# A hybrid encoder step: ten of eleven down steps of the FFN by seven block products instead of eight

## What is computed

```
h = rmsnorm(x)                              # norm2_g
a = h @ w_up                                # 1024 -> 2 * 2816
a = causal_depthwise_conv(a, width 3)       # prompt and each sample by itself
gate, up = split(a)
x = x + (silu(gate) * up) @ w_down          # 2816 -> 1024
```

## Time and profile before

| | us |
|---|---|
| three runs | 3447.86, 3453.91 (median), 3458.95 |
| profiled execution | 3453.28 |
| its span | 3451.5 |
| mean granted clock of PE | 0.965 |

### The profile page before, as it was taken

The page is one execution under the profiler, slowest core; times in us unless marked ns, Lnnn a source line. Parts: engine busy times, 40 slices in busy tenths (PEclk is TensorE's granted clock), DMA queues, the critical chain, the costliest instruction groups (busy, mean ns, idle before and its releaser), DMA issues. The chain is left out here.

```text
span 3451.5 us, 56818 instructions
## 1 busy us (share of the span) xinstructions
PE 3243.1 (94%) x23942; PEld 3039.6 (88%) x23942; DVE 2001.9 (58%) x3541; ACT 902.0 (26%) x1655; POOL 887.2 (26%) x782
## 2 busy tenths in 40 slices
PE   7999997889999999999988999979899999999997
PEld 5988975779999999999988898648799999999996
DVE  6396564562655565555666855546537655555556
ACT  3244244243211111111233431532332111111112
POOL 3221110223322222222342212011243222222223
PEclk9999998799999999999999999979999999999998
DMA  5633231101111111111164322320011111111111
GB/s 189 193 95 109 85 111 59 67 18 43 42 40 41 43 43 37 44 43 43 36 185 145 100 77 87 112 102 9 29 42 43 43 37 44 43 43 43 37 43 66
DMA packets 123430, 234.13 MB, mean 68 GB/s; under 512 B 34020, under 2 KB 84452, under 8 KB 119848
## 3 DMA queue, kind: packets, MB, share of 16 engines
q1 hardware_dynamic: 121096, 227.35, 20.3%
q10 hardware_dynamic: 2080, 3.15, 0.3%
HBM read 173.54 MB, written 54.43 MB: 66 GB/s over the span
## 5 line engine op out<-in xcount | busy, mean ns | idle before, releaser
L268 PE MATMUL PS<-h_split,w_split 128*128 128x384 f32 x3072 | 1062.4, 346 | 21.9 <-PEq L205 9.8
L270 PE MATMUL PS<-h_split,w_split 128*128 128x384 f32 x3072 | 1041.0, 339 | 0.0
L269 PE MATMUL PS<-h_split,w_split 128*128 128x384 f32 x3072 | 1037.2, 338 | 0.0
L263 POOL TENSOR_TENSOR w_split<-w_full,w_split 128x1024 fp32r<-128x1024 f32 (+1 forms) x192 | 466.1, 2428 | 911.8 <-ACT w_split L255 911.8
L268 PEld LDWEIGHTS PS<-h_split,w_split 128*128 128x128 f32 x3072 | 583.6, 190 | 41.4 <-issue 16.3
L269 PEld LDWEIGHTS PS<-h_split,w_split 128*128 128x128 f32 x3072 | 580.6, 189 | 2.5
L270 PEld LDWEIGHTS PS<-h_split,w_split 128*128 128x128 f32 x3072 | 580.2, 189 | 0.0
L255 ACT CAST w_split<-w_full 128x1024 fp32r<-128x1024 f32 (+1 forms) x194 | 202.0, 1053 | 1307.9 <-PE PS L270 1167.8
L2380 DVE TENSOR_TENSOR x<-x,PS 128x384 f32<-128x384 f32 x528 | 285.4, 551 | 160.2 <-PE PS L270 158.5
L268 PE MATMUL PS<-ffn_act,w_split 128*128 128x384 f32 x1056 | 366.1, 347 | 2.1 <-DVE w_split L2387 1.1
L269 PE MATMUL PS<-ffn_act,w_split 128*128 128x384 f32 x1056 | 356.0, 337 | 0.0
(11 more groups left out here) (398 smaller groups left out, 4912.2 us busy)
## 6 DMA issues: line engine op xcount, KB each, us to landing
w_full<-in_w_up SPq DMA_DIRECT2D x88, 512.0 KB, 3.2
w_full<-in_w_down SPq DMA_DIRECT2D x44, 512.0 KB, 3.2
...
kq_keep<-split_rows SPq DMA_DIRECT2D x128, 128.0 KB, 2.4
...
gdn_y<-y_keep SPq DMA_DIRECT2D x2, 3456.0 KB, 11.1
```

The lines of the kernel that those rows point to most:

```text
L263: pool.tensor_tensor(ws[:, n % SSLOTS, 1, 0:w], wf[:, n % WSLOTS, 0:w], ws[:, n % SSLOTS, 0, 0:w].bitcast(F32), ALU.subtract).then_inc(w_l ...
L268: pe.matmul(out, w_hi, a_hi, start=first, stop=False)
L269: pe.matmul(out, w_hi, a_lo, start=False, stop=False)
L270: return pe.matmul(out, w_lo, a_hi, start=False, stop=last)
```

## The change

The down product of a group q, 256 inputs (two tiles e) to 1024 outputs over 1152 tokens, is cut into two "mixes" h of 512 outputs. In a mix the weights are a 2 x 2 block matrix (rows: two halves of 256 outputs; columns: the two input tiles) and the activations another (rows: the two input tiles; columns: two halves of 576 tokens). Strassen's scheme in Winograd's form gives the four output blocks from seven block products: 4 weight blocks or sums thereof (S1 to S4 beside A11, A12, A22) and of activations (T1 to T4 beside B11, B21, B22). A step of a mix is one of the seven products for one of two output tiles p of 128 features: 2 halves of 288 columns in a pair of banks x 3 matmuls. So a mix has 14 steps and 84 matmuls of 288 columns. Products that share partial sums stay in their banks: m6 is added onto m1, m7 onto both, m4 onto all, m3 onto m5. After each step DVE adds the pair of banks (576 columns) to the block of x that needs it. There are three pairs, banks 4-5, 6-7 and 2-3, the last lent by the up tiles. The plain form stays for the last group (its product goes to `a2`, in the place of the then unused `h_split`).

The two mixes of group q-1 stand behind the second and the third up tile of group q (those of the tenth group at the end, before the two plain down tiles). Split weight tiles have two slots in place of three; a mix's split weights have 7 blocks of 256, high and low, in the room of slots 1 and 2. POOL forms the four weight sums, ACT copies seven high blocks, POOL writes seven low ones. Weights are split one tile ahead and not two: in POOL's list `weight_sums` and `lo` of tile n+1 stand behind its copies of tile n-1. DVE forms T1 to T4 (576 columns each; T1 after the first product of the group, the other three after the second), ACT and DVE split all seven activation blocks, two at a time after the first and the second product of the group. The product is written in two pieces (1024 and 128 columns), and the last low part of the weights moves from DVE to POOL.

The diff, cut, with half its indentation; regions, names and the counts of semaphores are left out:

```diff
-  tiles, ups = [], 0
-  for q in range(parts + 1):
-    downs = [("down", q - 1, 2 * q - 2), ("down", q - 1, 2 * q - 1)] if q >= 1 else []
-    for i in range(4 if q < parts else 0):
-      if i == 3 and q < parts - 1:
-        tiles += downs
-      tiles.append(("up", ups, (i % 2) * FF_TILES + 2 * q + i // 2))
-      ups += 1
-    if q >= parts - 1:
-      tiles += downs
-  return tiles, ups
+  tiles = []
+  for q in range(parts):
+    mixes = [("mix", q - 1, h) for h in range(2)] if q >= 1 else []
+    for i in range(4):
+      tiles.append(("up", 4 * q + i, (i % 2) * FF_TILES + 2 * q + i // 2))
+      if mixes and i in (1, 2):
+        tiles.append(mixes[i - 1])
+  last = parts - 1
+  tiles = [t for t in tiles if t[0] != "mix" or t[1] < last - 1]
+  tiles += [("mix", last - 1, h) for h in range(2)]
+  tiles += [("down", last, 2 * last + e) for e in range(2)]
...
+      kind, q, t = f_tiles[n - FFN_W]
+      if kind == "mix":
+        return d["w_down"][l, 2 * q:2 * q + 2, :, 512 * t:512 * t + 512].rearrange("e p c -> p e c"), KD * P
...
+    def slot_of(n):
+      return n % SSLOTS if n < FFN_W else 2 * ((n - FFN_W + 1) % 2)
...
+        STEPS = (("m1", 0, 0), ("m5", 0, 1), ("m1", 1, 2), ("m6", 0, 0), ("m3", 0, 1), ("m6", 1, 2), ("m7", 0, 0),
+            ("m2", 0, 1), ("m7", 1, 2), ("m4", 0, 0), ("m5", 1, 1), ("m4", 1, 2), ("m2", 1, 0), ("m3", 1, 1))
+        BANKS = (4, 6, 2)
...
+        def slot_free(eng, n):
+
+          if n < 2:
+            return
+          kind, c, t = tiles[n - 2]
+          if kind == "up":
+            eng.wait_ge(upr, NB * (c + 1))
+          else:
+            eng.wait_ge(dnr, M_STEPS * (2 * c + t + 1))
+          if mix_weights(n) is mix_w[1] if tiles[n][0] == "mix" else tiles[n][0] == "down":
+            eng.wait_ge(upr, NB * ups)
...
+          w, raw = mix_weights(n), wf[:, (FFN_W + n) % WSLOTS, 0:KD * P].rearrange("p (i c) -> p i c", c=256)
+          act.wait_ge(wsm, 2 * tiles[n][1] + tiles[n][2] + 1)
+          act.copy(w[0][:, A11], raw[:, 0])
+          act.copy(w[0][:, A12:A22 + 1], raw[:, 2:4])
+          act.copy(w[0][:, S1:S4 + 1], w[2][:, S1:S4 + 1]).then_inc(w_hid, 1)
...
+        def weight_sums(pool, link, n):
+
+          slot_free(pool, n)
+          pool.wait_ge(w_loaded[(FFN_W + n) % WSLOTS], 16 * ((FFN_W + n) // WSLOTS))
+          w, raw = mix_weights(n)[2], wf[:, (FFN_W + n) % WSLOTS, 0:KD * P].rearrange("p (i c) -> p i c", c=256)
+          link(pool.tensor_tensor(w[:, S1], raw[:, 1], raw[:, 3], ALU.add))
+          pool.tensor_tensor(w[:, S3], raw[:, 0], raw[:, 1], ALU.subtract)
+          link(pool.tensor_tensor(w[:, S2], w[:, S1], raw[:, 0], ALU.subtract))
+          pool.tensor_tensor(w[:, S4], raw[:, 2], w[:, S2], ALU.subtract).then_inc(wsm, 1)
...
+          pool.wait_ge(w_hid, FFN_W + n + 1)
+          pool.tensor_tensor(w[1][:, A11], raw[:, 0], w[0][:, A11].bitcast(F32), ALU.subtract)
+          pool.tensor_tensor(w[1][:, A12:A22 + 1], raw[:, 2:4], w[0][:, A12:A22 + 1].bitcast(F32), ALU.subtract)
+          pool.tensor_tensor(w[1][:, S1:S4 + 1], w[2][:, S1:S4 + 1], w[0][:, S1:S4 + 1].bitcast(F32),
+                   ALU.subtract).then_inc(w_lod, 1)
...
+            elif kind == "mix":
+              k = 2 * c + t
+              w = mix_weights(n)
+              pe.wait_ge(w_lod, FFN_W + n + 1)
...
+              for i, (name, p, s) in enumerate(STEPS):
+                if i == 2:
+                  pe.wait_ge(upf, 1 + max(u for u in range(units) if u % 4 in (2, 3)))
+                if i < 3 and k >= 1:
+                  pe.wait_ge(added, M_STEPS * (k - 1) + (13, 14, 12)[i])
+                if i >= 3:
+                  last_use = max(j for j in range(i) if STEPS[j][2] == s)
+                  pe.wait_ge(added, M_STEPS * k + last_use + 1)
+                a, b = MIXED[name]
+                fresh = name in ("m1", "m2", "m5")
+                for j in range(2):
+                  out = PS[:, BANKS[s] + j, 0:HALF // 2]
+                  cols = slice(HALF // 2 * j, HALF // 2 * (j + 1))
+                  w_hi, w_lo = (w[e][:, a, p * P:(p + 1) * P] for e in range(2))
+                  pe.matmul(out, w_hi, a7[:, 0, b, cols], start=fresh, stop=False, skip_group_check=True)
+                  pe.matmul(out, w_hi, a7[:, 1, b, cols], start=False, stop=False, skip_group_check=True)
+                  mm = pe.matmul(out, w_lo, a7[:, 0, b, cols], start=False, stop=True,
+                         skip_group_check=True)
+                mm.then_inc(dnr, 1)
+            elif tiles[n - 1][0] == "down":
...
+            behind = tiles[n + 1:n + 2] if n >= 1 and kind != "down" else []
+            for next_kind, *_ in behind:
+              if next_kind == "mix":
+                weight_sums(pool, link, n + 1)
+            for _ in behind:
+              lo(pool, n + 1)
...
-            lo(pool, n + 2)
...
+        def highs_early(act, q):
+
+          act.wait_ge(afl, 2 * q + 1)
+          if q >= 1:
+            act.wait_ge(dnr, 2 * M_STEPS * q)
+          act.copy(a7[:, 0, B11], au[:, 0:HALF])
+          act.copy(a7f[:, T3], au[:, HALF:TOK]).then_inc(ahi, 1)
+          act.wait_ge(asm, 2 * q + 1)
+          act.copy(a7[:, 0, T1], a7f[:, T1])
+          act.copy(a7f[:, T2], a7f[:, T1]).then_inc(ahi, 1)
+
+        def highs_late(act, q):
+
+          act.wait_ge(afl, 2 * q + 2)
+          act.copy(a7[:, 0, B21:B22 + 1], halves(au[:, 0:TOK])).then_inc(ahi, 1)
+          act.wait_ge(asm, 2 * q + 2)
+          act.copy(a7[:, 0, T3:T4 + 1], a7f[:, T3:T4 + 1]).then_inc(ahi, 1)
...
+          def product(j):
+            dve.wait_ge(cvd, 2 * j + 2)
+            dve.wait_ge(sld, j + 1)
+            dve.tensor_tensor(au[:, 0:SEQ], ag[:, 0:SEQ], au[:, 0:SEQ], ALU.mult)
+            dve.tensor_tensor(au[:, SM].rearrange("p (b i) -> p b i", b=DEC_BATCH),
+                     sample_view(ag, FFN_TAPS, 0, DEC_SEQ), sample_view(au, FFN_TAPS, 0, DEC_SEQ),
+                     ALU.mult).then_inc(afl, 1)
+
+          def sums_early(q):
+            dve.wait_ge(afl, 2 * q + 1)
+            if q >= 1:
+              dve.wait_ge(dnr, 2 * M_STEPS * q)
+            dve.tensor_tensor(a7f[:, T1], au[:, HALF:TOK], au[:, 0:HALF], ALU.subtract).then_inc(asm, 1)
+
+          def lows_early(q):
+            dve.wait_ge(ahi, 4 * q + 2)
+            dve.tensor_tensor(a7[:, 1, B11], au[:, 0:HALF], a7[:, 0, B11].bitcast(F32), ALU.subtract)
+            dve.tensor_tensor(a7[:, 1, T1], a7f[:, T1], a7[:, 0, T1].bitcast(F32), ALU.subtract).then_inc(alo, 1)
+
+          def sums_late(q):
+            dve.wait_ge(afl, 2 * q + 2)
+            dve.wait_ge(ahi, 4 * q + 2)
+            dve.tensor_tensor(a7f[:, T3], au[:, HALF:TOK], a7f[:, T3], ALU.subtract)
+            link(dve.tensor_tensor(a7f[:, T2], au[:, HALF:TOK], a7f[:, T2], ALU.subtract))
+            dve.tensor_tensor(a7f[:, T4], au[:, 0:HALF], a7f[:, T2], ALU.subtract).then_inc(asm, 1)
+
+          def lows_late(q):
+            dve.wait_ge(ahi, 4 * q + 4)
+            dve.tensor_tensor(a7[:, 1, B21:B22 + 1], halves(au[:, 0:TOK]), a7[:, 0, B21:B22 + 1].bitcast(F32),
+                     ALU.subtract)
+            dve.tensor_tensor(a7[:, 1, T3:T4 + 1], a7f[:, T3:T4 + 1], a7[:, 0, T3:T4 + 1].bitcast(F32),
+                     ALU.subtract).then_inc(alo, 1)
+
...
+          ADD_TO = {"m1": (0, 0), "m6": (0, 1), "m7": (1, 1), "m4": (1, 0), "m5": (1, 1), "m3": (0, 1), "m2": (0, 0)}
+
+          def mix_adds(q, h, between=iter(())):
+            k = 2 * q + h
+            for i, (name, p, s) in enumerate(STEPS):
+              dve.wait_ge(dnr, M_STEPS * k + i + 1)
+              for j, (other, other_p, _) in enumerate(STEPS[:i]):
+                if other_p == p and ADD_TO[other] == ADD_TO[name]:
+                  dve.wait_ge(added, M_STEPS * k + j + 1)
+              xs = halves(x_part(h, p, *ADD_TO[name]))
+              dve.tensor_tensor(xs, xs, mixed_out(s), ALU.add).then_inc(added, 1)
+              next(between, None)
...
+          for q in range(LAST + 1):
+            c = 4 * q
+            if q == 0:
               take(c)
-              conv = convolve(c, t)
-              if tiles[n + 1][0] == "up":
-                for _ in conv:
-                  pass
-            elif tiles[n - 1][0] == "down" and tiles[n - 1][1] == c:
-              for u in range(c * KD * NB, (c + 1) * KD * NB):
-                if u == LAST * KD * NB:
-                  last_low()
-                next(conv, None)
-                add(u)
-                m, b = down_unit(u)
-                if c == LAST and b == 1 and m == 5:
-                  invert_next(0)
-                if c == LAST and b == 2:
-                  next_row(m)
-              assert next(conv, None) is None
+            else:
+              convolve_tile(c - 1)
+              product(2 * q - 1)
+              sums_late(q - 1)
+              take(c, range(NB - 1))
+              lows_late(q - 1)
+              take(c, range(NB - 1, NB))
+            convolve_tile(c)
+            take(c + 1)
```

(13 more changed lines are left out.)

216 lines of the change are left out of this document (125 added, 91 removed).

## The result

The changed kernel takes 3468.1 us (median; 3465.7 to 3474.2, 7 runs) where the kernel before, on the same chip, takes 3456.1: a ratio of 1.0036, 95% interval 1.0026 to 1.0046. The forecast was 3426 us, 27 less than before; the kernel was measured at 12 more. A slower kernel had been given a chance of 0.18, and the measured time lies at the very end of the range, 3390 to 3469. Run again on another chip, beside two of the experiments, the changed kernel gave 1.0031, 1.0018 to 1.0044.

What follows compares the result with a forecast made beforehand. The prediction took PE's number of matmuls times their pitch as the bound. Its terms, -30.5 - 5.9 + 15.3 + 6.2, gave -14.9 us a layer, -30 for both, shaded by 3: from 3453.3 to 3426 us, range 3390 to 3469.

Steps and rivals of the forecast that it cites:

- Matmuls: Down product on PE: ten steps of 25.27 us become 20 mixes of 11.11, a gain of 30.5 us a layer.
- rival D: Mix matmuls: fewer columns don't pay because of a large fixed part; break-even 0.150 us at 288 columns; chance 0.01.
- Old stalls: Inside the old down steps: about 0.65 us a group of waiting goes, nine groups, a gain of 5.9 us a layer.
- term 5: First mix of each group: POOL's last low weights come 1.7 us late, nine times, a loss of 15.3 us a layer.
- Adds: DVE's 576-column adds in the mixes: 0.75 us each, about 0.67 start to start, covered by PE, cost nothing.
- term 4: ACT and DVE: ACT copies 4608 columns a group instead of 2304, DVE works some 9 us more; throughput no bound.
- The end: Layer's last two mixes and down step: stalls of 10.9 us against 4.7 now, a loss of 6.2 us a layer.
- rival B: Before each first mix: late weights make it slower, losing from 3.4 us of lateness; 3468.5 us at 4.2; chance 0.14.
- two signs of a wrong theory: On PE: waiting for adds inside mixes 0 to 17, or up tiles waiting for `take`, would show the prediction wrong.

Runs made afterwards that it cites:

- experiment 4: The changed kernel with each add of a mix taking only 288 of its 576 columns: 3464.3 us, ratio 1.0025 to the kernel before.
- Experiment 10: The changed kernel with the first up tile's last block taken on VectorE ahead of the two long low parts: 3472.5 us, ratio 1.0041 to the kernel before.
- experiment 3: The changed kernel with 18 unused matmuls on PE before the first mix of each group but the last: 3463.5 us, ratio 1.0021 to the kernel before.
- Experiment 1: The changed kernel with POOL's first-mix weight sums begun when PE ends the first up tile, ahead of POOL's copies: 3418.4 us, ratio 0.9891 to the kernel before.
- experiment 2: The changed kernel with the last weight sum formed three times in first mixes: 3538.2 us, ratio 1.0232 to the kernel before.

## Why the prediction was wrong

It named the right mechanism and got the sign wrong. By its own steps, per layer, where it had -14.9 us and the stage shows +7.2 (the mean of 7.6 and 6.7), a miss of 22.1:

1. *Matmuls*: -30.5 forecast. With 0.1345 us in place of 0.1323, 20 mixes of 84 take 226.0, ten down steps took 252.7: -26.7. Mis-sized by 3.8. The line through 256 and 384 columns was drawn from matmuls of other stages at its lower end, and 1.6% on the pitch of 1680 matmuls is as much as a whole term. That a 288-column matmul pays at all (rival D) is settled: 0.1345 is far under 0.150. By the prediction's estimate from two figures of the Trainium skill, TensorE: Matmul & The Clock Gate, § Back-to-back issue gap, this term would have been a loss (of 6.4 us a layer, as the two products of that estimate differ by 0.64, and not of 7). The trace disagrees: its pitch is 0.1345 us at 288 columns and 0.1757 at 384, where that line gives 0.102 and 0.114.
2. *Old stalls*: -5.9 as forecast. In the mixes 0 to 17 PE never waits for an add, and the boundaries between tiles cost nothing, but for the one of term 5. (The two figures that it subtracts differ by 0.73 and not 0.65; the starts of the old down steps give 0.6.)
3. *Adds*: as forecast, 754 ns each, hidden; experiment 4 shows it.
5. *Weights of the first mix*: +15.3 forecast, 9 x 2.65 = +23.9 measured. This is the step that failed by most, 8.6 of the 22.1. Its working has "two lows of 1152, 2.6" and "a wait for ACT's copy 0.3". The sums T3, T2 and T4 are three blocks of 576, so both ScalarE's copy and VectorE's second low run over 1728 columns, 1.65 and 1.95 us. The count goes wrong in term 4 already, which has ScalarE copy 4608 columns a group; the kernel copies 5184, one block of 576 more. VectorE thus stood idle for 0.78, not 0.3, and from its first low to the next take it needed 3.15, not 2.6; the convolution, held by POOL's low part, the sums and the takes had already cost 0.6 more. Together 1.6 us: the sums start at T+4.5 and not T+2.9. The 0.5 set aside for semaphores and 0.1 in the rest of the chain took back a part, and 1.0 more of lateness is left. That these three pieces make the difference is read from the trace; no run shortens the lows. Experiment 10, which takes them out of the chain ahead of the take, starts the sums only 0.5 sooner, because POOL's copies meet them then. What was taken for the meetings, sums 1.1 to 1.3 us apart in turns with the convolution, came out: 4.4 us for the four, 4.8 forecast.
   *No term at all* stood for the clock: +5.5 by the stretches, 5.0 by experiment 3. The prediction read a clock of 1.00 in the stage before and kept it without a reason, although its own term 5 has PE idle for 1.7 us, nine times, where before it is hardly ever idle. Whether 1.7 us would have been enough to bring the clock down, no run shows: behind 0.5 us it never fell, behind 2.65 it did.
6. *The end*: +6.2 forecast, beside the pitch of term 1. From the first start of mix 18 at 1680.2 to the last of the down step at 1742.0 are 61.8 us, 22.6 + 25.3 of them pitch: 13.9 of stall, against 4.7, so +9.2. The stall within the two mixes was given as 9.4 and is 9.9, so its working holds, the clock's share included. The down step was given 1.5 and has 4.0: 1.3 for the last low part, as written, and 2.0 around the four matmuls of the next stage's sums of squares. The trace of before has the same 2.0 there. The prediction took them off with the old 4.7 and left them out of its new 10.9.

The sum of these, -26.7 - 5.9 + 23.9 + 5.5 + 9.2, is +6.0, where 7.2 are measured; 1.2 are not assigned.

So rival B's outcome is what happened, though not by its number: the measured lateness of 2.65 lies within the 1 to 2.8 us that the chances give to the forecast. The prediction put the point of no gain at 3.4 us; told of 2.65, it would still have said faster. With the measured terms that point is lower: (26.7 + 5.9 - 9.2) / 9 = 2.6 without the clock, and (23.4 - 5.5) / 9 = 2.0 with all of it. No single term turns the sign clearly. With term 5 at its 15.3 the measured sum would be -2.6 us a layer, 5 over the run and less than these runs can tell from nothing; only if the clock had then held too would it be -8.1. Experiment 1, the changed kernel and experiment 2 show how the stage follows the gap: gaps of 0.69, 2.83 and 4.81 us, stages of 829, 854 and 885. Of the 24.8 us between the first two, 19.3 are gap (9 x 2.14) and 5.5 the clock; from the second to the third the step is steeper, as every first mix then meets the lower clock.

Most of what the prediction said would show it was there: the wait for the low part nine times a layer, the sums about 1.2 us apart from the second on, the adds at 0.75, some 9 us of waiting in mix 18. Neither of its two signs of a wrong theory appeared. What it had given as sizes did not come: 0.1345 us and not 0.132 in a mix, 2.65 and not 1.7 before it, a group of 76.4 us and not 74.6. Its signs tested where the time goes, not how much. Between the 1.7 us of the forecast and the 2.0 to 2.6 at which the change stops paying lay 0.3 to 0.9 us, and the hand sum over a dozen operations on three engines was off by 1.0.
